# Two-block transformer kernel: every dense pass of 512 tokens as two passes of 256

## The chip, the cores and the metric

The kernel runs on one core of a Trainium2 chip. The metric is device time in microseconds (us); lower is better. A run of the kernel before took 2321.73 us (median of three, 2320.89 to 2324.02).

## The reference

The computation is two transformer blocks in a row on one sequence of 512 tokens with 1024 features, all in float32. The first block is applied with two layers of weights, the second with one. What matters here are the dense products; each is tokens times a weight matrix:

```python
z = h @ w_in[l]                        # 1024 -> 4808 columns: queries, keys, values, index, gates
qb = (cq @ b_w_uq[l]); kv = (ckv @ b_w_ukv[l])
merged = gate_a * (y_a @ w_proj_a[l]) + gate_b * (y_b @ w_proj_b[l])
x = x + merged @ w_out[l]
u = causal_dwconv(h @ w_up[l], ...)    # 1024 -> 5632
x = x + (silu(gat) * val) @ w_down[l]  # 2816 -> 1024
```

The second block has the same parts (`w_in`, `w_out`, `w_gate`, `w_up`, `w_down`), with a compressed, a selected, a windowed and a dilated attention between them. Softmax, top-k selection, rotary turns and norms stand between the dense products.

## The kernel before, in words

Activations lie transposed, with features on the 128 partitions and the 512 tokens along the free axis. A weight matrix is cut into blocks of 128 by 128. Eight blocks are one tile of the stream: 512 KB, brought by SyncE's queue into a ring of four slots (`weight_ring`).

**Split operands.** A float32 product is made of three products of split operands. GpSimd splits each weight tile into an upper part `w_hi` (line 1993) and a rest `w_lo` (line 1999), both of type fp32r; VectorE and ScalarE split the activations in the same way into `arena_r`. TensorE's helper `matmul` (lines 527 to 535) then issues, for each block, lower weight times upper activation, upper weight times lower activation, and upper times upper, all three accumulating into the same PSUM tile. I call one of these three instructions a pass. Each pass is one MATMUL of up to 512 columns of the moving operand, preceded by its own LDWEIGHTS (weight load) of 128 by 128 for the stationary operand.

**Who calls it.** `linear` and `linear_pair` take weights as the stationary operand and the activations as the moving one (512 tokens wide). `token_major` has it the other way round: a block of 128 tokens is stationary and the four weight blocks are moving, 512 wide (280 wide for the values of the second block). The first four products of each layer of the first block (`qi`) are 384 tokens wide. The feed-forward loops (lines 926 and 1092) call it directly, and so do the 16 steps of the compressor in the second block (`hidden_steps`), whose passes are 256 columns wide. Its last products (`compressed`) are 64 columns wide.

**What sets the order.** TensorE's program is written out in order; each of the three feed-forward stages has two loops (`pe.Fori`) whose round computes two pairs of output tiles. At the first block of a weight tile TensorE waits for `weights_split`, and the first MATMUL on that tile increments `weights_begun`, which GpSimd waits for before it overwrites the other pair of split buffers. At an output tile's first block TensorE waits until one of its four PSUM banks has been emptied (`tile_taken`); its last pass increments `tile_done`, for which ScalarE or VectorE waits. Attention scores, transposes and probability-times-value products (lines 684, 704, 877, 1063 and others) don't go through the helper.

## Time and profile before

| | |
|---|---|
| median of three runs | 2321.73 us |
| the profiled execution's own time | 2322.03 us |
| its span (first to last instruction) | 2320.1 us |
| granted TensorE clock, mean | 0.998 of full speed |
| TensorE matmul (PE), busy | 2275.7 us, 98%, 11106 instructions |
| TensorE weight load (PEld), busy | 1769.7 us, 76%, 11106 instructions |
| GpSimd (POOL), busy | 1621.2 us, 70% |
| VectorE (DVE), busy | 1028.9 us, 44% |
| ScalarE (ACT), busy | 607.4 us, 26% |
| DMA | 212.62 MB, mean 92 GB/s |

PE and PEld are two rows for one engine: a weight load may run beside the matmul before it. The duration of one MATMUL in the trace includes the way through the array, so that successive matmuls overlap in the record: a pass of 512 columns is shown with some 395 ns, although the next one starts much sooner. What a pass costs is therefore read from the distance between starts, or from a long stretch divided by its number of passes. In lists "x18" is the number of instructions merged into a row, and the time beside the start is how long the merged row lasts.

### The profile page before, as it was taken

Reading aid. Unit: us, or ns where it says so; the run is one execution under the profiler, and the core shown is the slowest. Engines: PE = TensorE matmul, PEld = TensorE weight load, DVE = VectorE, ACT = ScalarE, POOL = GpSimd, SP = SyncE. Lnnn points to the kernel's source line nnn. Section 1 sums busy time; section 2 is a strip of 40 time slices with the busy share of each in tenths; the row PEclk is TensorE's granted clock in tenths of the full one; section 3 lists DMA queues with packets and bytes.
Section 4 is the critical chain, followed back from the end, with each engine's and each line's share of the span. In section 5 each row is a group of like instructions: output and inputs, shape, how many; then the busy total and the mean of one; then the engine's idle time right before and its main releaser. Section 6 shows DMA issues by size and latency. Waiting matters only on the chain.

```text
span 2320.1 us, 34416 instructions
## 1 busy us (share of the span) xinstructions
PE 2275.7 (98%) x11106; PEld 1769.7 (76%) x11106; DVE 1028.9 (44%) x2012; ACT 607.4 (26%) x1299; POOL 1621.2 (70%) x942
## 2 busy tenths in 40 slices
PE   7999999999999999999999999999999999999997
PEld 5666788878888876667888788888787777888886
DVE  5676644364214346775433643143544544110112
ACT  4334710231001232347102311012321853000001
POOL 6565577777777775655777777777766757777775
PEclk9999999999999999999999999999999999999999
DMA  6222023323232232220233223323372102323222
GB/s 210 73 74 101 20 91 91 100 85 97 91 98 93 91 102 64 79 104 20 82 99 92 91 90 95 95 90 99 130 222 91 34 22 95 92 91 100 90 91 90
DMA packets 61584, 212.62 MB, mean 92 GB/s; under 512 B 6344, under 2 KB 6728, under 8 KB 61328
## 3 DMA queue, kind: packets, MB, share of 16 engines
q1 hardware_dynamic: 54368, 194.38, 26.7%
q10 hardware_dynamic: 7088, 16.58, 2.1%
q8 instruction: 75, 1.23, 0.2%
q14 instruction: 53, 0.43, 0.1%
HBM read 208.78 MB, written 10.01 MB: 94 GB/s over the span
## 4 chain that ended last, share of the span: by engine, by line
PE 94%; DVE 2%; DVEq 1%; ACT 1%; POOL 1%; issue 1%; DMA 0%; ACTq 0%; SPq 0%; POOLq 0%
PE out_tile L531 79%; PE stat L704 3%; PE turned L684 2%; PE out_tile L877 2%; PE out_tile L1063 1%; PE stat L531 1%; PE out_tile L886 1%; PE out_tile L771 1%; DVEq L1540 1%; PE stat L684 1%; PE turned L657 1%; POOL w_lo L1999 1%; PE out_tile L895 0%; POOL w_hi L1993 0%; PE stat L623 0%
## 5 line engine op out<-in xcount | busy, mean ns | idle before, releaser
L531 PE MATMUL out_tile<-arena_r,w_hi 128*128 128x512 f32 (+1 forms) x5240 | 1641.0, 394 | 0.0
L531 PEld LDWEIGHTS out_tile<-arena_r,w_hi 128*128 128x128 f32 x5240 | 985.4, 188 | 230.5 <-issue 1.9
L531 PE MATMUL out_tile<-arena_r,w_lo 128*128 128x512 f32 (+1 forms) x2620 | 1042.6, 398 | 9.1 <-POOL w_lo L1999 6.6
L1993 POOL TENSOR_TENSOR w_hi<-weight_ring,cst 128x1024 fp32r<-128x1024 f32 x342 | 645.0, 1886 | 539.3 <-PE out_tile L531 473.7
L1999 POOL TENSOR_TENSOR w_lo<-weight_ring,w_hi 128x1024 fp32r<-128x1024 f32 x342 | 823.0, 2406 | 26.9
L531 PEld LDWEIGHTS out_tile<-arena_r,w_lo 128*128 128x128 f32 x2620 | 493.0, 188 | 151.4 <-issue 25.7
L1519 DVE TENSOR_TENSOR x<-out_tile,x 128x512 f32<-128x512 f32 x72 | 49.8, 691 | 360.1 <-PE out_tile L531 360.1
L1337 ACT ACTIVATE work<-out_tile,p 128x512 f32<-128x512 f32 x88 | 65.9, 774 | 410.2 <-PE out_tile L531 410.2
L1787 DVE SCALAR_TENSOR_TENSOR work<-out_tile,p,work 128x511 f32<-128x511 f32 x88 | 65.6, 745 | 222.9 <-ACT work L1337 222.9
L2038 POOL TENSOR_SCALAR work<-work,small 128x384 f32<-128x384 f32 (+3 forms) x108 | 56.1, 532 | 64.0 <-DVE small L1571 45.0
L1208 ACT ACTIVATE work<-work,small 128x384 f32<-128x384 f32 (+3 forms) x152 | 83.3, 559 | 37.0 <-DVE small L1564 37.0
L1564 DVE CUSTOM_DVE_ANT_0 work<-out_tile,arena 128x384 f32<-128x384 f32 (+3 forms) x152 | 69.1, 489 | 43.0 <-PE out_tile L886 14.0
L1431 ACT ACTIVATE work<-out_tile 128x512 f32<-128x512 f32 x22 | 13.2, 598 | 281.4 <-PE out_tile L531 281.4
L1135 ACT ACTIVATE arena_r<-x,p 128x512 fp32r<-128x512 f32 x48 | 34.6, 721 | 183.7 <-DVE x L1519 183.7
L704 PE MATMUL stat<-arena 128*64 128x128 f32 x1120 | 73.5, 278 | 5.8 <-DVE arena_r L1453 4.9
L1319 ACT ACTIVATE work<-out_tile,p 128x512 f32<-128x512 f32 x32 | 22.0, 689 | 210.3 <-PE out_tile L531 210.3
L531 PE MATMUL out_tile<-w_hi,arena_r 128*128 128x512 f32 (+1 forms) x256 | 76.6, 374 | 0.0
L704 PEld LDWEIGHTS stat<-arena 128*64 128x64 f32 x1120 | 60.0, 136 | 18.2 <-issue 13.7
L1201 ACT ACTIVATE arena<-turned 128x512 f32<-128x512 f32 (+1 forms) x112 | 54.7, 541 | 54.5 <-PE turned L684 53.4
L1758 DVE TENSOR_TENSOR work<-out_tile,work 128x512 f32<-128x512 f32 x14 | 9.7, 691 | 110.2 <-PE out_tile L531 110.2
L1655 DVE MAX8 small<-arena 128x8 f32<-128x256 f32 (+2 forms) x96 | 53.7, 559 | 5.9 <-issue 1.2
L531 PEld LDWEIGHTS out_tile<-w_hi,arena_r 128*128 128x128 f32 x256 | 46.3, 188 | 13.1 <-issue 5.1
(226 smaller groups left out, 1920.7 us busy)
## 6 DMA issues: line engine op xcount, KB each, us to landing
weight_ring<-stream SPq DMA_DIRECT2D x356, 512.0 KB, 3.5
arena<-bias_rows ACTq DMA_DIRECT2D x4, 2048.0 KB, 11.1
bias_rows<-bias_kept ACTq DMA_DIRECT2D x2, 2556.0 KB, 24.1
bias_rows<-bias_kept SPq DMA_DIRECT2D x1, 2556.0 KB, 15.0
x<-x_t SPq DMA_DIRECT2D x4, 512.0 KB, 9.2
arena<-w ACTq DMA_DIRECT2D x1, 2048.0 KB, 8.0
out_t<-arena SPq DMA_DIRECT2D x8, 256.0 KB, 2.2
cst<-consts SPq DMA_DIRECT2D x1, 576.0 KB, 14.2
```

The lines of the kernel that those rows point to most:

```text
L531: ins = pe.matmul(out, l, r, start=start and n == 0, stop=stop and n == 2, **kw)
L684: ins = pe.transpose(turn_bank(j)[:, at + k * P:at + (k + 1) * P], share(g, parts[j])[:, k * P:(k + 1) * P], ident)
L704: ins = pe.matmul(bank[e * HD:(e + 1) * HD, b * P:(b + 1) * P], values(group, e, k), turned[:, at:at + P], start=(opens(group) and not ope ...
L1201: act.activation(turned[:, at:at + width], turn_bank(j)[:, 0:width], ACT.Copy)\
L1208: act.activation(share(g, part), share(g, part), ACT.Exp, scale=-1.0, bias=negmax[:, c:c + 1], accum_out=rsum[:, c:c + 1]).then_inc(sec.ex ...
L1337: act.activation(work[:, s, :], psum[(n0 + s) % 4][:, :], ACT.Identity, scale=p1[:, bass.ds(c + 2, 1)], bias=p1[:, bass.ds(c + 3, 1)])\
L1564: dve.tensor_tensor_reduce(share(g, part), score_bank(j, group), bias(group, part), 1.0, 3e38, ALU.add, ALU.min, negmax[:, c:c + 1]).then_ ...
L1655: dve.max(top8, s)
L1787: dve.scalar_tensor_tensor(out=work[:, s, 1:S], in0=ps[:, 0:S - 1], scalar=p1[:, bass.ds(c + 1, 1)], in1=work[:, s, 1:S], op0=ALU.mult, op ...
L1993: pool.tensor_tensor(blocks_of(w_hi[:, s % SPLIT, :], used), blocks_of(ring[:, s, :], used), cols(cst, C_ONE).unsqueeze(1).to_broadcast([P ...
L1999: pool.tensor_tensor(blocks_of(w_lo[:, s % SPLIT, :], used), blocks_of(ring[:, s, :], used), blocks_of(w_hi[:, s % SPLIT, :].bitcast(F32), ...
L2038: pool.tensor_scalar(share(g, part), share(g, part), rinv[:, c:c + 1], scale, ALU.mult, ALU.mult)\
```

## The change

In the helper `matmul`, an output that is 512 wide is now computed in two halves of 256 columns: first the three products of the first 256 columns (tokens, or weight columns in `token_major`), then the three products of the other 256. Outputs of any other width are left as they were (`qi` at 384, the values of the second block at 280, the compressor at 256 and 64). Every half pass has its own LDWEIGHTS, so one block that had three loads and three matmuls has six and six. The number of columns streamed and the products computed stay the same. The flag `start`, which resets the accumulation of a bank, is set on the very first pass alone, and `weights_begun` is still incremented by the first pass and `tile_done` by the last.

```diff
+        token_halves = (slice(0, S // 2), slice(S // 2, S))
...
             def matmul(out, lhs, rhs, start, stop, **kw):
-                for n, (l, r) in enumerate(((lhs[1], rhs[0]), (lhs[0], rhs[1]), (lhs[0], rhs[0]))):
-                    ins = pe.matmul(out, l, r, start=start and n == 0, stop=stop and n == 2, **kw)
-                    if state["begin"]:
-                        ins.then_inc(weights_begun, 1)
-                        state["begin"] = False
+                halves = token_halves if out.shape[-1] == S else (slice(0, out.shape[-1]),)
+                if len(halves) > 1:
+                    kw["skip_group_check"] = True
+                for h, at in enumerate(halves):
+                    for n, (l, r) in enumerate(((lhs[1], rhs[0]), (lhs[0], rhs[1]), (lhs[0], rhs[0]))):
+                        ins = pe.matmul(out[:, at], l, r[:, at], start=start and n == 0 and h == 0, stop=stop and n == 2, **kw)
+                        if state["begin"]:
+                            ins.then_inc(weights_begun, 1)
+                            state["begin"] = False
                 return ins
```

TensorE's program at the head of the feed-forward loop of the first block, before. `w_lo` and `w_hi` are the split weights, loaded as stationary operand; `arena_r` is the moving one; the last figures are the size of the output; "waits" names the semaphores that hold an instruction.

```order
L926 UNCONDITIONAL_BRANCH
L926 ISA
L549 REGISTER_ALU [waits one_tile_taken_v]
L531 MATMUL out_tile<-arena_r,w_lo 128x512 [waits weights_split]
L531 MATMUL out_tile<-arena_r,w_hi 128x512 x2
L932 REGISTER_ALU
L531 MATMUL out_tile<-arena_r,w_lo 128x512 [waits one_tile_taken_v]
L531 MATMUL out_tile<-arena_r,w_hi 128x512 x2
```

The same place on TensorE now:

```order
L932 UNCONDITIONAL_BRANCH
L932 ISA
L555 REGISTER_ALU [waits one_tile_taken_v]
L537 MATMUL out_tile<-arena_r,w_lo 128x256 [waits weights_split]
L537 MATMUL out_tile<-arena_r,w_hi 128x256 x2
L537 MATMUL out_tile<-arena_r,w_lo 128x256
L537 MATMUL out_tile<-arena_r,w_hi 128x256 x2
L938 REGISTER_ALU
L537 MATMUL out_tile<-arena_r,w_lo 128x256 [waits one_tile_taken_v]
L537 MATMUL out_tile<-arena_r,w_hi 128x256 x2
L537 MATMUL out_tile<-arena_r,w_lo 128x256
L537 MATMUL out_tile<-arena_r,w_hi 128x256 x2
```

Each block's three passes have become six narrower ones; the waits stand where they stood, on the first pass of the block.

The second place is TensorE in the token-major values of the first block, before. Here the weights are the moving operand and `arena_r` the stationary one:

```order
L549 REGISTER_ALU
L558 REGISTER_ALU [waits weights_split]
L531 MATMUL out_tile<-w_hi,arena_r 128x512 [waits one_tile_taken_a]
L531 MATMUL out_tile<-w_lo,arena_r 128x512
L531 MATMUL out_tile<-w_hi,arena_r 128x512
```

And now:

```order
L555 REGISTER_ALU
L564 REGISTER_ALU [waits weights_split]
L537 MATMUL out_tile<-w_hi,arena_r 128x256 [waits one_tile_taken_a]
L537 MATMUL out_tile<-w_lo,arena_r 128x256
L537 MATMUL out_tile<-w_hi,arena_r 128x256 x2
L537 MATMUL out_tile<-w_lo,arena_r 128x256
L537 MATMUL out_tile<-w_hi,arena_r 128x256
```

Again three have become six under the same waits. The other engines' programs are the same as before.

## Rows read from the trace of the kernel before

**Rows 1.** The page: PE's busy time, the granted clock, the chain by engine.

```profile
PE 2275.7 (98%) x11106; PEld 1769.7 (76%) x11106; DVE 1028.9 (44%) x2012; ACT 607.4 (26%) x1299; POOL 1621.2 (70%) x942
...
PEclk9999999999999999999999999999999999999999
...
PE 94%; DVE 2%; DVEq 1%; ACT 1%; POOL 1%; issue 1%; DMA 0%; ACTq 0%; SPq 0%; POOLq 0%
```

**Rows 2.** The chain in order of time: start, length (us), what, instructions.

```profile
282.34 182.19 PE out_tile L531 x780
487.43 346.76 PE out_tile L531 x1485
...
1761.13 19.95 PE out_tile L531 x87
...
1939.30 366.81 PE out_tile L531 x1572
```

**Rows 3.** Groups by form, PE: form, count, busy us, mean ns, idle before, releasers.

```profile
L531 PE MATMUL out_tile<-arena_r,w_hi 128*128 128x512 f32 x5112 | 1607.1, 395 | 0.0
L531 PE MATMUL out_tile<-arena_r,w_lo 128*128 128x512 f32 x2556 | 1018.8, 399 | 4.4 <-POOL w_lo L1999 1.9 <-DVE work L1795 1.0 <-DVE arena_r L1546 0.7
...
L531 PE MATMUL out_tile<-w_hi,arena_r 128*128 128x512 f32 x192 | 63.7, 400 | 0.0
L531 PE MATMUL out_tile<-w_lo,arena_r 128*128 128x512 f32 x96 | 37.6, 392 | 0.0
...
L531 PE MATMUL stat<-w_hi,arena_r 128*128 128x512 f32 x32 | 11.0, 406 | 0.0
...
L531 PE MATMUL stat<-w_lo,arena_r 128*128 128x512 f32 x16 | 6.3, 392 | 0.0
...
L531 PE MATMUL stat<-arena_r,w_hi 128*128 128x512 f32 x16 | 5.0, 395 | 0.0
...
L531 PE MATMUL stat<-arena_r,w_lo 128*128 128x512 f32 x8 | 3.4, 421 | 0.0
```

**Rows 4.** Groups by form, PEld: the loads of the passes.

```profile
L531 PEld LDWEIGHTS out_tile<-arena_r,w_hi 128*128 128x128 f32 x5240 | 985.4, 188 | 230.5 <-issue 1.9
```

**Rows 5.** Timeline of PE, the compressor's passes of 256 columns: start, length (us).

```profile
1703.48 2.32 PE L531 MATMUL stat<-arena_r 128*128 128x256 f32 x18
1705.63 0.40 PE L531 MATMUL out_tile<-arena_r,w_lo 128*128 128x512 f32 x1
...
1711.24 3.74 PE L531 MATMUL stat<-arena_r 128*128 128x256 f32 x30
1714.81 0.40 PE L531 MATMUL out_tile<-arena_r,w_lo 128*128 128x512 f32 x1
```

**Rows 6.** Timeline of PEld beside the first of them.

```profile
1703.60 1.99 PEld L531 LDWEIGHTS stat<-arena_r 128*128 128x128 f32 x16
1705.52 0.19 PEld L531 LDWEIGHTS out_tile<-arena_r,w_lo 128*128 128x128 f32 x1
```

**Rows 7.** Timeline of PE, passes of 64 columns.

```profile
1727.53 1.08 PE L531 MATMUL turned<-arena_r 128*128 128x64 f32 x9
1728.45 0.48 PE L531 MATMUL out_tile<-arena_r,w_lo 128*128 128x512 f32 x1
```

**Rows 8.** Timeline of PE, passes of 384 and 280 columns.

```profile
30.14 0.34 PE L531 MATMUL out_tile<-arena_r,w_lo 128*128 128x384 f32 x1
...
31.70 0.34 PE L531 MATMUL out_tile<-arena_r,w_lo 128*128 128x384 f32 x1
...
1702.84 0.29 PE L531 MATMUL out_tile<-w_lo,arena_r 128*128 128x280 f32 x1
...
1703.22 0.29 PE L531 MATMUL out_tile<-w_lo,arena_r 128*128 128x280 f32 x1
```

**Rows 9.** Timeline of PE behind small products (L1004): two neighbouring starts.

```profile
1735.22 0.50 PE L531 MATMUL out_tile<-arena_r,w_lo 128*128 128x512 f32 x1
1735.56 0.63 PE L531 MATMUL out_tile<-arena_r,w_hi 128*128 128x512 f32 x2
```

**Rows 10.** Stretch of attention: busy us and count of each engine.

```profile
1800.00:1880.00 80.00, 78.76 (x776) 57.88 (x774) 48.52 (x208) 69.34 (x219) 54.37 (x87) 1.00 0.05 16
```

**Rows 11.** Waits of PE: us in total, times, longest.

```profile
PE out_tile L531 <- POOL w_lo L1999: 6.6, 8, 2.0
```

**Rows 12.** The page, costliest groups: GpSimd's two split operations.

```profile
L1993 POOL TENSOR_TENSOR w_hi<-weight_ring,cst 128x1024 fp32r<-128x1024 f32 x342 | 645.0, 1886 | 539.3 <-PE out_tile L531 473.7
L1999 POOL TENSOR_TENSOR w_lo<-weight_ring,w_hi 128x1024 fp32r<-128x1024 f32 x342 | 823.0, 2406 | 26.9
```

## The prediction, made before the changed kernel ran

> **What bounds the kernel now.** I read the page first: PE is busy for 98% of the span, the granted clock stands at full speed (2.4 GHz) in every slice, and 94% of the chain that ended last is PE [rows 1]. So the question is what TensorE does per pass, and the next view is the same chain in order of time. The reader is to see there that line 531, the dense helper, fills unbroken stretches of hundreds of microseconds, in which nothing but the distance between passes counts: 346.76 us for 1485 passes is 233.5 ns each, 366.81 for 1572 is 233.3, 182.19 for 780 is 233.6; with the weights as the moving operand 19.95 us for 87 is 229.3 [rows 2]. 512 columns at 2.4 GHz are 213.3 ns, so a pass costs 20 ns (16 ns) more than its columns. Third, the groups by form give the number of passes 512 columns wide: 5112 + 2556 + 16 + 8 = 7692 with activations moving, 192 + 96 + 32 + 16 = 336 with weights moving, 8028 in all [rows 3]. At 233.4 and 229.3 ns they take 1872 us, 81% of the span. The mean duration in those rows (395 ns) is no cost, as passes overlap in the record.
>
> Each pass has a load of 128 columns, recorded with 188 ns [rows 4]. It lies under a pass of 233 ns whole. Whether it still does under a pass of 256 columns is what the change turns on.
>
> **The change, part by part.**
>
> Removed: 8028 passes of 512 columns, 7692 at 233.4 ns and 336 at 229.3 ns. Added: 16056 passes of 256 columns, each with its load. The trace of before has this very form, from the same line: three-product accumulations into one bank, 256 fp32r columns moving, a 128x128 load of its own for each. 18 of them start at 1703.48 and the next pass at 1705.63: 2.15 / 18 = 119.4 ns. 30 of them from 1711.24 to 1714.81: 119.0 ns [rows 5]. The loads under the first run come at 1.92 us for 16, which is 120.0 ns [rows 6]. The first few passes of a run are a bit faster than the rest (the mean over 30 is below the steady 120), and a dense stage is nearly all steady state. I take 120 ns, 240 for a pair.
>
> How far can it be off? From below, the load alone doesn't hold it under 112: nine passes of only 64 columns, with the same load, start 0.92 / 9 = 102 ns apart on average over that row [rows 7], the first of them bunched behind the pass before, so the floor of the load is near 100 to 112 and a 256 pass sits above it. The columns alone are 106.7 ns. Passes of 384 columns come at 1.56 / 9 = 173.3 ns, of 280 at 0.38 / 3 = 126.7 [rows 8]; both scaled down by columns give 115.6 and 115.8. So a pair costs between 231.4 and, since a pass of 256 will hardly be slower than one of 280, 253.4 ns. I choose 240, as it is the only one measured at 256 columns, twice.
>
> The sum: 7692 x (240 - 233.4) = +50.8 us, 336 x (240 - 229.3) = +3.6 us, together +54.4. None of it lies beside other work that could hide it: the stretches of rows 2 are the chain itself.
>
> The weights that would be late aren't. A weight tile of eight blocks takes GpSimd 1886 + 2406 ns = 4.3 us [rows 12]; TensorE uses it in 24 passes x 233.4 = 5.6 us now and 48 x 120 = 5.76 after. GpSimd's slack grows by 0.16 us a tile. Of TensorE's waits, those for `w_lo` sum to 6.6 us in 8 places [rows 11]; where they stem from GpSimd being just behind, a slower TensorE gives some back. I take half, -3 us; the ends are 0 and -6.6.
>
> Semaphores: no wait and no increment is added; the first half pass carries the waits, the last the signal. Where a pass waits, its load can't go ahead: behind small products two starts are 340 ns apart, 107 more than a dense pass [rows 9]. That happens once at such a place and will happen once there after, then in front of a half pass; it costs 107 ns before and after. A tile's end comes no later, as the last half drains through the array as before; the evictions by VectorE and ScalarE wait for TensorE, not the other way round. Cost 0.
>
> Issue rate: twice the instructions in the dense stages, one matmul and load every 120 ns. In attention TensorE already takes 776 matmuls in 80 us, one per 103 ns, held over the whole stretch [rows 10]. Cost 0. The feed-forward loops double in length, and their 24 jumps back (three stages of 4 + 4 jumps) don't show in the unbroken stretches now [rows 2]; with passes half as long there is half as much work in the queue to cover a jump. I take 0; at 1 us each it would be +24.
>
> Untouched are the passes of 384, 280, 256 and 64 columns and all of attention. Total against the profiled execution's own time: 2322.0 + 54.4 - 3 = 2373 us. That execution is 0.3 us from the median of the runs, so the same number holds for both: +2.2%.
>
> A page of the Trainium skill, "TensorE: Matmul & The Clock Gate", section "Back-to-back issue gap", has another price: a pass costs its columns at 2.4 GHz plus 2.5 ns, 215.8 for 512 and 109.2 for 256. By that a pair is only 2.6 ns dearer than a pass and the change costs an estimated 21 us (2343). The trace doesn't agree: it has 233 and 120, so the rule lacks some 18 and 11 ns.
>
> **The rivals.**
>
> A, the other side: the 20 ns above the columns grow with the columns, and nothing is fixed per pass. For it: 384 and 280 columns scale to 115.6 and 115.8 per 256, against 116.7 for half of 512; then a half pass is no dearer than half a pass, and the load is still hidden. Price: 7692 x (231.4 - 233.4) = -15.4, 336 x (231.4 - 229.3) = +0.7, and no waits given back: 2307 us, 0.6% faster. It decides if half passes come under 116.5 ns. Against it: 48 passes of exactly 256 columns came at 119 to 120, and their load was as long as here.
>
> B, a small fixed part: with weights moving, 512 columns cost 229.3 and 280 cost 126.7, a slope of 0.442 ns and 3.5 ns fixed. One more pass per pair then costs 3.5 ns, 28 us in all, less 2 given back: 2348 us. For it speaks that `w_hi` and `w_lo` are other buffers than the compressor's operands; against it, again the 48 passes.
>
> C, loads that come out from under: a load isn't pulled ahead in time when passes are this short, and 107 ns [rows 9] show in some of the added passes. In one of six it would be 2676 x 107 = 286 us on top of the sum, 2659 in all; at the jumps back alone, +24 (2397). Against it: in the compressor no pass of 48 shows it. The same page, section "Measured speedup vs the span model", says that a load overlaps with running matmuls only when it goes to another row group; by it every added load would show, an estimated 8028 x 107 = 859 us. Here the trace doesn't agree: all loads fill the 128 rows, and the passes stand 233 apart.
>
> That two halves with the same `w_hi` share a load, so that less is added, is excluded: now two passes in a row have the same `w_hi` too, and there are 5240 loads for 5240 such passes [rows 3, 4].
>
> **How the numbers follow.** The forecast, half passes at 119 to 121.5 ns (2357 to 2397 us): 0.73. B, 117.5 to 119 (2335 to 2357): 0.09. A: 0.09, of which 0.02 would end within 0.2%. C and anything dearer than 121.5: 0.09. 0.2% is 4.6 us, about what the runs can tell from no change. Faster 0.07, same 0.02, slower 0.91. The range runs from 2340 to 2400: it leaves out A, the cheapest part of B and the dear part of C, some 0.18.
>
> **What would show it.** Right: in long chain stretches of the dense line about 120 ns per pass (96 passes in 11.5 us), 19134 matmuls and as many loads, busy PE still near 98%, GpSimd's waits for TensorE longer, attention stretches as long as before. Wrong: 116 per pass (A), or gaps of 220 ns among the half passes (C), or gaps that come once per loop round. What would make the number wrong while the reason stands is a steady distance other than 120, each ns of which is worth 16 us.

## The result and the profile after

The changed kernel took 2294.8 us (median of 13 runs, 2289.26 to 2324.5), the kernel before 2322.17 us (13 runs, 2320.89 to 2324.02). The ratio is 0.989 with a 95% interval of 0.9877 to 0.9903: 1.1% faster, where I had forecast 2.2% slower. The ratio leaves out the run of 2324.5 us as a slow one, though its granted clock (0.998) is that of the others and more streams on the dearer side described below may explain it as well. Note the scatter: the kernel before varies by 3 us, the changed one by more than 25 even without that run. The profiled execution took 2306.57 us (span 2304.6), at the slow end of its runs.

The page of the changed kernel, against [rows 1]:

```profile
PE 2259.0 (98%) x19134; PEld 2125.9 (92%) x19134; DVE 1024.5 (44%) x2012; ACT 607.6 (26%) x1299; POOL 1624.0 (70%) x942
...
PEclk9999999999999999999999999999999999999999
...
PE 94%; DVE 2%; DVEq 1%; ACT 1%; POOL 1%; issue 1%; DMA 0%; ACTq 0%; SPq 0%; POOLq 0%
...
L1999 POOL TENSOR_TENSOR w_hi<-weight_ring,cst 128x1024 fp32r<-128x1024 f32 x342 | 647.9, 1894 | 520.0 <-PE out_tile L537 456.3
```

TensorE has the 19134 matmuls and loads that were foretold, full clock, and still makes up 94% of the chain. But GpSimd's waits for TensorE fell from 473.7 [rows 12] to 456.3 us: TensorE hands over its weight tiles faster than before.

The chain of the changed kernel in order of time (start, length, what, instructions) answers to [rows 2]:

```profile
279.96 177.01 PE out_tile L537 x1560
479.87 350.08 PE out_tile L537 x2970
...
1095.08 177.00 PE out_tile L537 x1560
1294.95 339.60 PE out_tile L537 x2994
...
1684.34 2.16 PE stat L537 x18
...
1692.15 3.60 PE stat L537 x30
1741.65 20.51 PE out_tile L537 x174
...
1920.83 369.83 PE out_tile L537 x3144
```

Divide each length by its count. The compressor's rows (`stat`) are at 120 ns, as before [rows 5]. The dense stages aren't: 113.5 ns in the first row, 117.9 in the second, 113.5 and 113.4 in the next two, 117.9 with weights moving, 117.6 in the last. The second and the fourth row are the same code on the same buffers, the feed-forward stage of the first block's two layers, 4.5 ns a pass apart. The windows of the profile (us, then PE busy, instructions in it, granted clock, DMA share, GB/s) show the two stages inside, where nothing waits:

```profile
500.00:820.00 320.00, 320.00 (x2720) 1.00 0.29 93
1300.00:1620.00 320.00, 320.00 (x2826) 1.00 0.30 97
```

A window counts passes that lie partly in it, some two more than start there: 117.7 and 113.3 ns. The clock is the same in both; DMA share and traffic (0.29 and 93 GB/s, 0.30 and 97) differ as the pace does.

The single distances show no mixture. Each unbroken stretch settles within about six passes after a stall on one of two distances and keeps it, once for 2968 passes (480 to 829 us): 113 and 114 ns in turn (mean 113.3, which I call low) or 117 to 119 (mean 117.8, high). A pair of half passes costs 226.7 low and 235.6 high, where one pass of 512 columns cost 233.4. In this trace some 8150 half passes are low and 7550 high; the mean over all is 115.5.

Where the time went, from the distances between the starts of neighbouring TensorE matmuls (us; a stall is what a distance has above an unhindered pass):

| | dense, 512 or 256 wide, less stalls | stalls in it | 384, 280, 64 wide | all else (attention, transposes, norms, compressor) |
|---|---|---|---|---|
| before | 1872.0 | 21.7 | 55.4 | 348.7 |
| after | 1854.7 | 25.0 | 54.9 | 348.8 |
| difference | -17.3 | +3.3 | -0.5 | +0.1 |

The sum is -14.4; the two profiled executions are 15.5 us apart, the rest (1.1 us) lies before the first matmul. The forms of the passes (count, busy us, mean ns, idle before) against [rows 3]:

```profile
L537 PE MATMUL out_tile<-arena_r,w_hi 128*128 128x256 f32 x10224 | 1773.2, 278 | 0.0
L537 PE MATMUL out_tile<-arena_r,w_lo 128*128 128x256 f32 x5112 | 1431.5, 280 | 4.6 <-POOL w_lo L2005 2.0 <-DVE work L1801 1.0 <-DVE arena_r L1552 0.8
L537 PE MATMUL out_tile<-w_hi,arena_r 128*128 128x256 f32 x384 | 71.4, 283 | 0.0
```

And TensorE's waits (total us, times, longest) against [rows 11]:

```profile
PE out_tile L537 <- POOL w_lo L2005: 6.5, 8, 2.1
...
PE out_tile L537 <- DVE arena_r L1516: 2.1, 1, 2.1
```

The 6.6 us of waits for `w_lo` are still 6.5. The second row is new, the one place with a visible new stall: where the first layer ends and the second begins. Timeline of TensorE in the changed kernel:

```profile
829.54 0.40 PE L537 MATMUL out_tile<-arena_r,w_hi 128*128 128x256 f32 x2
832.07 0.44 PE L537 MATMUL out_tile<-arena_r,w_lo 128*128 128x384 f32 x1 [2.14 <-DVE arena_r L1516]
```

and before:

```profile
833.56 0.63 PE L531 MATMUL out_tile<-arena_r,w_hi 128*128 128x512 f32 x2
834.27 0.44 PE L531 MATMUL out_tile<-arena_r,w_lo 128*128 128x384 f32 x1
```

The last of two half passes starts at about 829.66: 2.4 us until the next pass, where there were 0.475. It isn't chance: the 13 traces with split passes all have it (2.0 to 3.3 us), and the traces of the kernel before and of its variants with 512-wide passes have 0.2 to 0.6 us. The profile puts it down to VectorE; whether the jump back over the longer program plays a part I did not test.

### The profile page after: what moved, and what is told of

Read it like the earlier page. It is cut to its first block, busy times and chain, and to the rows that moved or that the text cites. A ratio compares the mean times of both kernels' runs of the same rounds, so it can differ in the third digit from the quotient of the medians.

```text
span 2304.6 us, 50472 instructions
## 1 busy us (share of the span) xinstructions
PE 2259.0 (98%) x19134; PEld 2125.9 (92%) x19134; DVE 1024.5 (44%) x2012; ACT 607.6 (26%) x1299; POOL 1624.0 (70%) x942
## 4 chain that ended last, share of the span: by engine, by line
PE 94%; DVE 2%; DVEq 1%; ACT 1%; POOL 1%; issue 1%; DMA 0%; ACTq 0%; SPq 0%; POOLq 0%
PE out_tile L537 79%; PE stat L710 3%; PE turned L690 2%; PE out_tile L883 2%; PE out_tile L1069 1%; PE stat L537 1%; PE out_tile L892 1%; PE out_tile L777 1%; DVEq L1546 1%; PE stat L690 1%; PE turned L663 1%; POOL w_lo L2005 1%; PE out_tile L901 1%; POOL w_hi L1999 0%; PE stat L629 0%
## 5 line engine op out<-in xcount | busy, mean ns | idle before, releaser
L537 PE MATMUL out_tile<-arena_r,w_hi 128*128 128x256 f32 (+1 forms) x10352 | 1806.9, 279 | 0.0
L537 PEld LDWEIGHTS out_tile<-arena_r,w_hi 128*128 128x128 f32 x10352 | 1576.4, 188 | 1.9 <-issue 1.9
L537 PE MATMUL out_tile<-arena_r,w_lo 128*128 128x256 f32 (+1 forms) x5176 | 1455.1, 281 | 11.2 <-POOL w_lo L2005 6.5
L1999 POOL TENSOR_TENSOR w_hi<-weight_ring,cst 128x1024 fp32r<-128x1024 f32 x342 | 647.9, 1894 | 520.0 <-PE out_tile L537 456.3
L537 PEld LDWEIGHTS out_tile<-arena_r,w_lo 128*128 128x128 f32 x5176 | 977.5, 189 | 37.9 <-issue 25.9
L537 PE MATMUL out_tile<-w_hi,arena_r 128*128 128x256 f32 (+1 forms) x448 | 84.3, 285 | 0.0
L537 PEld LDWEIGHTS out_tile<-w_hi,arena_r 128*128 128x128 f32 x448 | 69.8, 188 | 5.5 <-issue 5.1
L537 PE MATMUL out_tile<-w_lo,arena_r 128*128 128x256 f32 (+1 forms) x224 | 62.7, 280 | 0.0
## 6 DMA issues: line engine op xcount, KB each, us to landing
arena<-bias_rows ACTq DMA_DIRECT2D x4, 2048.0 KB, 10.9
```

Source lines behind the costliest of these rows:

```text
L537: ins = pe.matmul(out[:, at], l, r[:, at], start=start and n == 0 and h == 0, stop=stop and n == 2, **kw)
L1999: pool.tensor_tensor(blocks_of(w_hi[:, s % SPLIT, :], used), blocks_of(ring[:, s, :], used), cols(cst, C_ONE).unsqueeze(1).to_broadcast([P ...
```

## The experiments

Each text on record names its own theories by letters; the words after it say which it was.

**1. The changed kernel again**, no edit. Does the side (low or high) belong to the place in the program, or is it drawn in each execution?

> The changed kernel once more. In its first trace every unbroken stream of half passes settles within some six passes on one of two distances, 113.3 ns or 117.8 ns, and keeps it for up to 3000 passes; the feed-forward stage of layer 0 ran at 117.8, that of layer 1 at 113.3 with the same code and buffers. Theory P (phase): the first passes after a stall decide, so another execution has other stages at the low distance; each of the three feed-forward stages (about 3000 half passes) that changes moves the time by 13.4 us, and the time is 2270 to 2340 us. Rival S (stage): what runs beside a stage decides, so the same stages are low (280 to 457, 1095 to 1634 us) and the same high (480 to 830, 1937 to 2290), and the time is 2304 to 2310 us.

2299.09 us. The chain:

```profile
282.92 177.01 PE out_tile L537 x1560
482.83 336.90 PE out_tile L537 x2970
...
1287.45 339.61 PE out_tile L537 x2994
...
1913.34 369.83 PE out_tile L537 x3144
```

The stage with 350.08 us has 336.90 for the same 2970 passes: 113.4 ns. The same program, another side. So it is drawn per execution, and the scatter of the runs has its source. The chip alone doesn't decide it, as the ten runs of experiment 2, all on one chip, go from 2291.69 to 2322.96 us. It isn't a fair coin: the stages at 280 and 1095 us were low and the last one high in both traces. In experiment 14 the stage at 282 us was high, so that one isn't tied to its side; the last stage was high in every trace in which nothing was done about it.

**2. Products outer, halves inner.** The two halves of one product follow each other, and successive passes no longer add to the same 256 columns of PSUM.

```diff
-                for h, at in enumerate(halves):
-                    for n, (l, r) in enumerate(((lhs[1], rhs[0]), (lhs[0], rhs[1]), (lhs[0], rhs[0]))):
+                for n, (l, r) in enumerate(((lhs[1], rhs[0]), (lhs[0], rhs[1]), (lhs[0], rhs[0]))):
+                    for h, at in enumerate(halves):
```

> Each of the three products does its two halves in a row, so that successive passes accumulate into different columns of the bank and use the same weights twice in a row. Theory P: distances are again 113.3 and 117.8, mixed by chance, 2275 to 2330 us. Rival R (repeat): accumulating into the same 256 columns pass after pass is what costs the 4.5 ns (or, in the compressor, the 6.7 ns up to 120.0); then every stream of halves runs at 113.3 and the time is 2270 to 2277 us, while the compressor, which has one half only, stays at 120.

2313.71 us (10 runs, 2291.69 to 2322.96), ratio 0.9957 (0.993 to 0.9985). The trace, of one of its quicker executions, has low and high as before:

```profile
481.98 336.90 PE out_tile L537 x2970
...
1908.49 369.84 PE out_tile L537 x3144
```

113.4 and 117.6 ns. Returning to the same columns at once is not what makes a stretch high. The higher median suggests that this order draws high more often; with one trace that isn't shown.

**3. Thirds** (176, 168 and 168 columns), to find the floor that the load sets.

```diff
-        token_halves = (slice(0, S // 2), slice(S // 2, S))
+        token_halves = (slice(0, 176), slice(176, 344), slice(344, S))
```

> Three passes of 176, 168 and 168 columns in place of two of 256, each with its load. Theory F (load floor): a pass can't come sooner than its load lets it, 112 ns as at 64 columns; three take 336 ns against 233.4, so 8028 x 102.6 = +824 us, about 3145 us, with distances of 112 whatever the state. Rival C (columns): the distance goes with the columns alone, 17/16 of them as in the low state, 226.7 ns for three, 2268 to 2300 us.

3144.03 us.

```profile
335.28 261.46 PE out_tile L537 x2340
598.50 526.60 PE out_tile L537 x4716
```

111.7 ns in both, for 70 to 73 ns of columns: the columns don't set the distance but the load that each pass has, and low lies 1.6 ns above that floor. That it is the load and not the issue of two instructions a pass is argued, not tested; the trace of the kernel before speaks for it. Its scores (line 704), whose loads have 64 columns, come two passes in 109 ns, and its transposes (line 684), 128 columns wide with a 128x128 load each, come one in 109 ns. So 111.7 is the floor of these dense passes, not of every load of 128 columns. The Trainium skill, "TensorE: Matmul & The Clock Gate", section "LDWEIGHTS (loading the stationary operand)", gives a load of P columns P/1.2 ns, 107 for 128; the trace has 111.7.

**4. The first block of each output tile in passes of 512**, the rest in halves: do wide passes move a stretch from one side to the other?

```diff
-                halves = token_halves if out.shape[-1] == S else (slice(0, out.shape[-1]),)
+                halves = token_halves if out.shape[-1] == S and not start else (slice(0, out.shape[-1]),)
```

> The first block of every output tile is done in passes of 512 columns again, all other blocks in halves: about 960 of the 8028 wide passes stay whole, and the streams of halves in the feed-forward stages are begun anew at each tile. Theory P: each new beginning draws again, so the long stages are no longer all low or all high; runs lie within some 5 us of each other, around 2275 (all low) to 2338 (all high), about 2306 if both are as likely. If the step from 512 to 256 columns always ends in the same state, all stages are alike: 2275 or 2338. Rival S (stage): the low and high stages are those of the changed kernel, 2300 to 2310 us.

2308.95 us (5 runs, 2304.58 to 2326.06), ratio 0.994 (0.9923 to 0.9956). Of the trace's groups of three wide passes without a stall near, 64 went from low to high, 59 from high to low, 3 stayed high. Of groups of six, 76 stayed (72 high, 4 low). One flip in the timeline:

```profile
615.58 0.28 PE L537 MATMUL out_tile<-arena_r,w_lo 128*128 128x256 f32 x1
615.70 0.40 PE L537 MATMUL out_tile<-arena_r,w_hi 128*128 128x256 f32 x2
615.93 0.39 PE L537 MATMUL out_tile<-arena_r,w_lo 128*128 128x512 f32 x1
616.16 0.63 PE L537 MATMUL out_tile<-arena_r,w_hi 128*128 128x512 f32 x2
616.63 0.28 PE L537 MATMUL out_tile<-arena_r,w_lo 128*128 128x256 f32 x1
616.75 0.39 PE L537 MATMUL out_tile<-arena_r,w_hi 128*128 128x256 f32 x2
616.97 0.28 PE L537 MATMUL out_tile<-arena_r,w_lo 128*128 128x256 f32 x1
```

Ahead of the wide passes three halves take 350 ns (615.58 to 615.93), 117 each; behind them 340 (616.63 to 616.97), 113 each. So the side is a state that a stretch carries along, and other passes can change it. The three wide ones take 231, 229 and 236 ns out of high, 226, 236 and 231 out of low.

**5. One block of three wide passes ahead of the last feed-forward loop**, to send that stage, high in every trace so far, to the low side.

```diff
+                state["until_whole"] = state.get("until_whole", 0) - 1
+                whole = state["until_whole"] == 0
-                halves = token_halves if out.shape[-1] == S else (slice(0, out.shape[-1]),)
+                halves = token_halves if out.shape[-1] == S and not whole else (slice(0, out.shape[-1]),)
...
+                    state["until_whole"] = 2 * DC
                     linear_pair((("gate", 1), ("upp", 1)), h_ffn, DC, ready=LAYERS * 5 * DC + 3 * DC)
```

> The changed kernel with one block, the last one in front of the feed-forward loop of the second block, done in three passes of 512 columns. In all three traces of half passes the 3000 passes behind it run at 117.8 ns. Where single tiles had three 512-wide passes between halves, the state changed sides each time (high, then 231, 229, 236, then low; low, then 226, 236, 231, then high). Theory P (phase, turned by an odd number of 512-wide passes): the last stage now runs at 113.3 ns, 3000 x 4.45 ns = 13 us less than the changed kernel, median about 2282 us. Rival S (what runs beside a stage, or a new draw at the end of the interruption): the last stage stays at 117.8 and the time is 2295 us; if it is drawn anew, runs of both kinds appear.

2308.57 us (6 runs, 2292.94 to 2314.48), ratio 0.9928 (0.9905 to 0.9952): no better than the change alone. In the trace the stage stayed high:

```profile
484.02 350.08 PE out_tile L539 x2970
...
1927.88 369.83 PE out_tile L539 x3141
```

The wide passes took 235, 236 and 231 ns here, not 231, 229 and 236; one of the three groups of experiment 4 that stayed high took 236, 236 and 231 too. High is thus more than one alignment, and my rule that three wide passes always change the side fell.

**6. Uneven halves** (264 and 248), whose average is the same as before.

```diff
-        token_halves = (slice(0, S // 2), slice(S // 2, S))
+        token_halves = (slice(0, 264), slice(264, S))
```

> 264 + 248 columns in place of 256 + 256. 248 columns at the low rate (17/16 of the columns) would be 109.8 ns, below the floor of 112 that loads set. Theory F (floor ends the state): a pass that waits for its load takes away the phase, so all streams run at 112 + 116.9 = 229 ns a pair whatever the start: 2285 to 2290 us and runs within 4 us of each other. Rival P (states as before): pairs of 227 to 236 by chance, runs from 2290 to 2325 us.

2358.88 us (4 runs, 2358.58 to 2359.18), ratio 1.0158 (1.0143 to 1.0172).

```profile
284.68 185.66 PE out_tile L537 x1560
493.23 353.38 PE out_tile L537 x2970
```

119.0 ns a pass in both, 238 a pair against the 229 expected, and the scatter is gone. The same columns in the same number of passes cost 1.6% more than before and 2.8% more than in even halves. That alone refutes a price per column.

**7, 8, 12, 13, 16. Why is the compressor at 120?** All in the kernel before; they change only the compressor's 48 passes. 7: stationary operand replaced by the constant `ident_r`. 8: moving operand replaced by the activations `h_mix`. 12: outputs alternate between two column ranges. 13: all waits gathered ahead of the first pass. 16: both operands replaced.

```diff
-                    ins = matmul(hidden, (blocks_hi[:, k, :], blocks_lo[:, k, :]),
+                    ins = matmul(hidden, (ident_r[:, :], ident_r[:, :]),
```
```diff
-                                 (w1_hi[:, k // 2, at], w1_lo[:, k // 2, at]), start=(k == 0), stop=(k == 15))
+                                 h_mix(k // 2, slice(0, 2 * P)), start=(k == 0), stop=(k == 15))
```
```diff
-                    ins = matmul(hidden, (blocks_hi[:, k, :], blocks_lo[:, k, :]),
+                    ins = matmul(stat[0][:, k % 2 * 2 * P:k % 2 * 2 * P + 2 * P], (blocks_hi[:, k, :], blocks_lo[:, k, :]),
```
```diff
-                    pe.wait_ge(w1_ready, k // 2 + 1)
+                    if k == first:
+                        pe.wait_ge(w1_ready, 8)
```
```diff
-                    ins = matmul(hidden, (blocks_hi[:, k, :], blocks_lo[:, k, :]),
-                                 (w1_hi[:, k // 2, at], w1_lo[:, k // 2, at]), start=(k == 0), stop=(k == 15))
+                    ins = matmul(hidden, (ident_r[:, :], ident_r[:, :]),
+                                 h_mix(k // 2, at), start=(k == 0), stop=(k == 15))
```

> The kernel before (512-wide passes) with one thing changed in the compressor's 48 passes of 256 columns: their stationary operand is the constant identity (ident_r), from its own buffer, in place of the blocks in arena_r; the compressor's result is therefore not computed. Theory O (operands): 120.0 ns comes of loading from the same arena that the moving operand streams from; the distances become 113.3 or 117.8. Rival (phase): 120.0 is a third state that this place starts in, and stays.

> As the run before it, but the stationary blocks are the compressor's own and the moving operand is the normed input (h_mix) in place of the compressor's first-layer weights; its result is not computed. Theory O (operands): if the place of the moving operand is what costs 120.0, the distances become 113.3 or 117.8. Rival (phase): they stay at 120.0. If both runs stay at 120.0, neither operand's place is the cause.

> The kernel before, with the compressor's blocks accumulated in turn into the first and the second 256 columns of the bank; its result is not computed. Theory R (repeat): its 48 passes leave 120.0 for 113.3 or 117.8. Rival (phase): they stay at 120.0, as they did with another stationary and with another moving operand.

> The kernel before, with the waits for the compressor's weights (w1_ready) gathered: one wait for all of them at the first of the six steps and one at the first of the ten, in place of one wait a step. Theory W (waits): in the compressor each block's first pass carries a semaphore wait, and a load that has to look at a semaphore, even one long met, can't go as far ahead; that holds the passes at 120.0 ns. Without them they run at 113.3 or 117.8. Rival (phase): 120.0 is a third steady distance that this place happens to start in; it stays.

> The kernel before, with both operands of the compressor's 48 passes of 256 columns exchanged at once: the constant identity as stationary, the normed input (h_mix) as moving operand; its result is not computed. Theory O2 (each of the two operands alone can hold the passes at 120.0): with both gone they run at 113.3 or 117.8. Rival: they stay at 120.0, and the operands are out.

In all five the passes stayed at 120.0 ns (mean over the 48 119.3 in 7), and the times were 2322.07, 2322.4, 2324.76, 2322.41 and 2321.95 us. Neither operand alone, nor both in these replacements, nor the columns, nor the waits explain the compressor's distance. Nor does the stream ahead of it. The row of 18 passes always follows passes of 280 columns and reads 2.15 or 2.16 us. The row of 30 follows passes of 512 before, high half passes in most later traces and low ones in experiment 10, and its steady distance is 120 in all of them. But the compressor does choose the side of what follows: in the seven traces where nothing but half passes follows it, they are high at once behind both rows, 14 times of 14.

**9. Only the first product of each tile's first block 512 wide.**

```diff
+                products = ((lhs[1], rhs[0]), (lhs[0], rhs[1]), (lhs[0], rhs[0]))
+                order = [(n, slice(0, out.shape[-1])) for n in range(3)]
+                if out.shape[-1] == S:
...
+                    whole = 1 if start else 0
+                    order = order[:whole] + [(n, at) for at in token_halves for n in range(whole, 3)]
+                for i, (n, at) in enumerate(order):
...
```

> At the first block of every output tile the first of the three products is one pass of 512 columns, all else is in halves. In the run with three 512-wide passes there, 123 of 126 undisturbed groups of three changed the side (low to high 64, high to low 59) and 76 of 76 groups of six kept it. Theory T (each 512-wide pass turns the phase by half): one pass changes the side too, so the long stages alternate tile by tile between 113.3 and 117.8, runs agree within 5 us, about 2300 us (halves at 115.5 on average, 1872 down to 1849 us in the dense stream, and 320 wide passes). Rival K (only a group of three does it, because it moves the place within the block's three products): sides are kept, and the time scatters as in the changed kernel, 2290 to 2325.

2338.51 us (4 runs, 2337.45 to 2341.49), ratio 1.0068 (1.0051 to 1.0084). Neither theory as I had put it: behind a single wide pass with no stall near the stream was high in 131 of 134 cases, whatever it was before (125 stayed high, 6 came from low, 3 ended low).

```profile
282.41 183.82 PE out_tile L540 x1518
489.13 350.05 PE out_tile L540 x2915
...
1955.58 370.00 PE out_tile L540 x3086
```

The three stages contain some wide passes of 235 ns, which make the mean 120 to 121; the half passes among them are at 117.8. The dense passes take 1886.1 us in all, near the 1891 that 8028 pairs at 235.6 would.

**10. The first two products of each tile's first block 512 wide**: the same edit with a 2.

```diff
-                    whole = 1 if start else 0
+                    whole = 2 if start else 0
```

> Two 512-wide passes at the first block of every output tile. Theory T: an even number keeps the side, so the long stages are all low or all high from their start, 2280 to 2335 us with scatter. Rival M (the high state has several alignments to the block's three products, and a group of two moves from one to the next while the low state, which has none, is kept): after a few tiles every stage is low and stays there, 2274 us without scatter, which would be the fastest version.

2285.74 us (4 runs, 2284.41 to 2286.89), ratio 0.9842 (0.9826 to 0.9859): 1.6% faster than before, 0.5% faster than the change, and the scatter is 2.5 us. Behind two wide passes with nine unhindered half passes on either side the stream was low in 124 of 124 cases, 9 of which came from high. In the gate and up stages two tiles start together, so that two such pairs stand close; behind them it was low in 76 of 76. Where TensorE had waited at the pair itself, it was high 17 times. The chain, every stage low:

```profile
483.63 337.61 PE out_tile L540 x2860
...
1286.81 340.36 PE out_tile L540 x2880
...
1911.89 357.36 PE out_tile L540 x3028
```

A correction in the timeline, as it comes when a tile starts:

```profile
493.96 0.39 PE L540 MATMUL out_tile<-arena_r,w_lo 128*128 128x512 f32 x1
494.18 0.63 PE L540 MATMUL out_tile<-arena_r,w_hi 128*128 128x512 f32 x3
494.65 0.39 PE L540 MATMUL out_tile<-arena_r,w_lo 128*128 128x512 f32 x1
...
495.35 0.28 PE L540 MATMUL out_tile<-arena_r,w_lo 128*128 128x256 f32 x1
495.46 0.39 PE L540 MATMUL out_tile<-arena_r,w_hi 128*128 128x256 f32 x2
495.69 0.28 PE L540 MATMUL out_tile<-arena_r,w_lo 128*128 128x256 f32 x1
```

(A merged row bears its first pass's shape; the row of three holds one wide pass and two halves.) 495.35 to 495.69 is 340 ns for three halves. Rival M was right in kind, but 2274 us had been expected. The dense passes take 1830.8 us, where all of them low would be 8028 x 226.7 = 1819.9. Of the 10.9 us between, 3 are the price of the wide passes (in 352 places a half and two wide ones take 113 + 226 + 236 = 575 ns, 8.5 more than five low halves), and some 8 are halves that ran high from a stall to the next such place. Against before (1872.0) the dense passes give -41.2 us, stalls +4.3 and the narrow passes +0.6; the medians are 36.1 us apart.

**11. Both halves of the last down product into the same 256 columns** (changed kernel).

```diff
-                        ins = pe.matmul(out[:, at], l, r[:, at], start=start and n == 0 and h == 0, stop=stop and n == 2, **kw)
+                        ins = pe.matmul(out[:, halves[0] if state.get("same") else at], l, r[:, at], start=start and n == 0 and h == 0, stop=stop and n == 2, **kw)
...
+                state["same"] = True
                 linear_tiles(lambda j: ("down", part, j), parts(*hid), n, LAYERS * FC + first, hid_done)
+                state["same"] = False
```

> The changed kernel, with both halves of the last block's down projection (1056 half passes) accumulated into the same 256 columns of the bank; that part of the result is not computed. Theory R (repeat): never leaving the 256 columns is what holds the compressor at 120.0 ns; these 1056 passes then run at 120.0 too, while the gate and up passes around them run at 113.3 or 117.8. Rival: they run at the distance of the passes around them.

2305.32 us; those passes came at 117.8, like the ones around them. With experiment 2 this ends the theory of the output columns.

**14. A wait that is already met ahead of every block of the last down product** (changed kernel).

```diff
+                if state.get("checked"):
+                    pe.wait_ge(load_first, 16)
...
+                state["checked"] = True
                 linear_tiles(lambda j: ("down", part, j), parts(*hid), n, LAYERS * FC + first, hid_done)
+                state["checked"] = False
```

> The changed kernel, with a wait that is met since the start (load_first) in front of every block of the last block's down projection (1056 half passes, six to a block). Theory W: a wait at every sixth half pass pulls these passes off 113.3 or 117.8, to 120.0 or to a mix with it, about 119 on average, against the gate and up passes around them. Rival: they run at the distance of the passes around them, as they did in same_columns.

2312.68 us; 117.8 with and without. Waits that are met don't make the 120 either.

**15. The two wide passes at every second tile start only**: is the price of experiment 10 worth halving?

```diff
-                    whole = 2 if start else 0
+                    state["starts"] = state.get("starts", 0) + bool(start)
+                    whole = 2 if start and state["starts"] % 2 else 0
```

> The two 512-wide passes at an output tile's start, which led every stream to 113.3 ns in the run with them at all tiles, now at every second tile's start only: 176 fewer groups, each of which cost some 8 to 13 ns more than its columns in halves. Theory M (a group of two always ends low and low is kept): the time falls by 2 us more, 2284 us, scatter below 4 us. Rival: streams begun at an unlocked tile draw the high side more often, and the time is 2288 us or more.

2285.7 us (4 runs, 2283.39 to 2287.62), ratio 0.9837 (0.9821 to 0.9854): the same as experiment 10. The stream was low behind all 137 groups without a stall near, and high behind 11 at which TensorE had waited.

**17. `ident_r` as the stationary operand of the last down product** (changed kernel): can an operand make 120 in a dense stage?

```diff
                     for n, (l, r) in enumerate(((lhs[1], rhs[0]), (lhs[0], rhs[1]), (lhs[0], rhs[0]))):
+                        if state.get("constant"):
+                            l = ident_r[:, :]
...
+                state["constant"] = True
                 linear_tiles(lambda j: ("down", part, j), parts(*hid), n, LAYERS * FC + first, hid_done)
+                state["constant"] = False
```

> The changed kernel, with the constant identity as stationary operand in the last block's down projection (1056 half passes); that part of the result is not computed. Theory O2: loading from another place than w_hi and w_lo moves these passes to 120.0 (or to the other side). Rival (side set by the start of the stream alone): they run at the distance of the gate and up passes around them.

2296.05 us. The windows of TensorE ahead of, in, between and in again the 1056 passes of the edit:

```profile
1960.00:2020.00 60.00, 60.00 (x512) 1.00 0.30 96
2045.00:2105.00 60.00, 60.00 (x503) 1.00 0.29 94
2120.00:2200.00 80.00, 80.00 (x682) 1.00 0.28 92
2230.00:2275.00 45.00, 45.00 (x377) 1.00 0.23 73
```

Less the two or so that lie partly outside: 117.7, 119.8, 117.7 and 120 ns. The single distances in the second and fourth are 120.0. The edit's own passes, and no others, stand at a third distance, and the stream returns to high behind them. The clock is 1.00 in all four windows, and the DMA share hardly differs in the first three (0.30, 0.29, 0.28). So what is loaded as the stationary operand (its place in memory, its content, or that it is the same for every pass, which this doesn't separate) can set the distance of a 256-column pass. Why the compressor stays at 120 with its own operands, and with the others tried, is still open.

## Why the prediction was wrong

**What bounds the kernel:** right. TensorE is 98% busy, 94% of the chain, at full clock, and the dense stages are unbroken streams. Attention, with all else outside the dense helper and with the compressor, took 348.8 us against 348.7.

**The cost of a half pass:** this step failed. I wrote "I choose 240, as it is the only one measured at 256 columns, twice". Measured were 226.7 and 235.6 a pair. I had matched the compressor's passes by shape, type and line; that their operands lie in other buffers I had named under rival B alone, and had not weighed. Experiment 17 shows that another stationary operand alone is worth 2.2 ns, from 117.8 to 120.0; 48 passes in two short runs beside one another were one case, not two. And I thought that a shape has one price. Experiments 1, 4, 9 and 10 show that it has at least two in the same code, and that neighbours choose which. The term of +54.4 us was -17.3 in the trace; at all high it would be +19, at all low -52. My lower bound of 231.4, scaled from 384 and 280 columns, was no bound: low pairs took 226.7. What keeps a stream on one distance or the other stays open.

**Given back by the waits for `w_lo`:** I took -3 us; they went from 6.6 to 6.5, nothing. TensorE didn't become slower, so the case never arose.

**Semaphores, issue rate, jumps:** 0 was right for the first two. Where a pass waits behind other work, the excess of some 104 ns over an unhindered one stands 73 times in the dense stages of the new trace (7.6 us) and 71 times in the old (7.4), as the step on semaphores said; another 60 distances of some 206 ns answer to 61 of some 320. The feed-forward loops' 24 jumps show nothing; the one between the layers shows a stall of 2.4 us instead of 0.475, its cause not settled.

**The forecast of 2373** was wrong in sign, and the range (2340 to 2400) lay above every run.

**Rival A** (a price by columns, 2307 us) named the right side and hit the profiled execution, but by chance. It expected 115.7 everywhere. The mean over the half passes of the trace, 115.5, is near it, but no stream ran there: it is a mixture of 113.3 and 117.8, the median over the runs is 2294.8, and uneven halves (experiment 6) contradict it. **Rival B** (117.5 to 119 a pass) fits the high side at 117.8 and misses the low one. Its sum was off too: a slope of 0.442 leaves 229.3 - 226.4 = 2.9 ns fixed, not 3.5, and some 2343 us, not 2348. **Rival C** (exposed loads) didn't occur: the 73 distances of some 220 ns in the dense stages answer to 71 of some 337 before, and even under passes of 168 to 176 columns the distance was 111.7. The sentence of the Trainium skill that the prediction set beside this rival stands in the section "The mechanism" of the page that it names. The Trainium skill's price for a half pass, in the section "Back-to-back issue gap" of the same page, is 109.2, and it calls that the gap of a single isolated matmul, without a load; by the traces even the low side stands 4 ns above it, and no stream of dense passes came below 111.7 on average, not even with a third of the 512 columns.

## What to carry to other kernels

A distance measured on one stream of instructions is the price of that stream, not of its shape: before scaling it to thousands, compare operands and neighbours as well as sizes, and give a range that spans all comparable rows. Where the load (here 111.7 ns) and the columns of a pass (106.7) took nearly the same time, the distance settled on several values, and a few passes of another width chose which: dividing long stretches by their counts shows it at once, and so does run-to-run scatter that the kernel before hadn't. If you narrow passes to this point, try a pair of wide ones at each tile's start (here worth 1.6% against the kernel before, 0.5% against halves alone), and time several executions.

## What the runs showed of the hardware

- The distance between passes with a 128x128 load of their own, fp32r, at full clock: 233.4 ns at 512 columns, 113.3, 117.8 or 120.0 at 256, 119.0 on average at 264 and 248 in turn, 111.7 on average at 168 to 176. Two halves can thus be cheaper than a whole (226.7 against 233.4).
- The side persists over thousands of passes (2968 in a row) and can change behind a stall, in the same code differently from execution to execution.
- With no stall near, one wide pass leads to high (131 of 134), two to low (124 of 124), three change the side (123 of 126), six keep it (76 of 76). The order of the products in a tile's first block differs between these kernels as well, so the number of wide passes may not be all of it.
- Passes at the third distance, 120 ns, leave the stream high behind them (14 of 14 behind the compressor, and in experiment 17).
- By what mechanism the alignments come about I can't say. The load's floor (111.7 ns) and the columns (106.7) are nearly equal here, and it is a guess that the two settle into one phase or the other; no run tested it by itself.
- The fastest version is that of experiments 10 and 15, at 2285.7 us, 1.6% under the kernel before.
